# Side units ahead of the attention scores, eight gate units of layer 1 moved into retention and attention, and units in three passes

## The chip, the cores and the metric

One core of a Trainium2 chip runs the whole program. The metric is the device time of one execution in microseconds (us). The engines named here are PE (TensorE, the matrix multiplier), DVE (VectorE), ACT (ScalarE) and SP (SyncE, which only issues DMAs). Each engine works through its own queue strictly in order and waits on semaphores for the others. Matmul results go to eight PSUM banks.

## The reference, cut to what matters

Two networks follow each other. The first has two mixer layers with four branches each; in layer 0 the 256 tokens and the 256 context tokens are both needed (512 columns), in layer 1 mostly the 256 tokens (256 columns). The second network has an RG-LRU block, a gated FFN, a gated linear attention block and another FFN.

```python
for l in range(DEPTH):                       # DEPTH = 2
    px = split_proj(hx @ w_in[l])            # ret_*, sc_*, cf_*, att_*, merge_gates
    ret_x = retention_bidir(ret_q, ret_k * k_scale, ret_v, ...)
    att_x = windowed_gqa(rope(att_q), rope(att_k), att_v, ...)   # softmax(scores) @ v
    r = head_group_norm(ret_x) * silu(ret_z)
    s = short_conv(sc_b, sc_c, sc_x) * silu(sc_z)
    f = conformer_conv(cf_glu) * silu(cf_z)
    a = att_x * silu(att_z)
    merged = sum(sigmoid(g) * (br @ w_branch[i])
                 for i, (g, br) in enumerate(zip(gates, (r, s, f, a))))
    x = x + gate_x * (merged @ w_out[l])
# second network
x = x + gt_m * rmsnorm(mixer(h)); x = x + gt_f * rmsnorm(conv_ffn(h))   # twice
```

The gate `sigmoid(g)` has 4 x 1024 columns, 1024 for each branch; they depend on nothing but the layer's normalized input `hx`, so they can be projected as early as that is there. All of it is float32.

## The kernel before

**Units.** Every large projection is cut into units of 128 output columns. The weights come in slabs of two units (`ring`, 3 slabs, one DMA by SP each, in the order of the list `stream`). A unit's weights are split into a rounded part and the rest: `w_hi` is a copy on ACT (L1115), `w_lo` is `slab - w_hi` on DVE (L1729), and there are four buffers of each (`PARTS`), so that the split of unit u waits until PE has used unit u-4. The input is split in the same way (`h_hi`, `h_lo`). PE then makes three products for each of 8 tiles k of the contraction: `w_hi·h_hi` (L537), `w_hi·h_lo` (L538), `w_lo·h_hi` (L539), 24 matmuls per unit, interleaved by k. `unit()` waits at the start for both `w_hi` and `w_lo` of the unit; `open_bank` waits until what was in that bank eight openings ago has been emptied; `project` (L547) is the two and the 24 matmuls. Some calls of `project` also pass `ready`, a wait before each k for an input that is only just being made. ACT and DVE split ahead of use: `split_until(name)` is three units past `name` (`AHEAD`), and is called at fixed places in their queues.

**Clock keepers.** `keep_clock(n)` (L506, matmul at L512) puts n dummy matmuls of ones, each counted twice in the profile, where PE would have nothing to do.

**Retention** (layer l, loops over 4 heads). PE: scores of head n (L716), a unit where `in_ret` names one (none in layer 1; `keep_clock(8)` at n = 1), then the output of head n-1 (L726, L732), which waits for the decayed scores that DVE makes (L2075).

**Attention.** Eight tiles of 128 queries and two heads in layer 1 (16 in layer 0). In step i of its loop PE does scores of tile i+1 (L757), the first side unit of the step, the output of tile i-2 (L780), further side units, `keep_clock(11)` in step 1 of layer 1, and the turning of tile i-1 (L768, eight transposes). ACT does the exponentials of tile i (L1368), which also empty its score banks; then for each side unit the split of a later unit (L1115) and the evacuation of this one (L1101); then the evacuation of the turned tile i-1 (L1101). DVE does the band and row maximum of tile i (L2095, L2100), the w_lo for the side units (L1729), the weights of tile i-1 (L2126), and the store of output i-3 (L2133). So PE turns tile i-1 when DVE has made its weights, for which ACT has to have made its exponentials.

**Side units** are units that nothing in the stage needs: `side_tiles` (L454) shares out sc_b, sc_z, ret_z and att_z. In layer 1 eight of them run before retention and eight inside attention, one in each of steps 1 to 8 and none in step 0. In layer 0 four are before or in retention and 12 in attention.

**Merge.** For each branch in `MERGE_ORDER` (sc, ret, att, cf) there are 4 pairs: two gate units, then two branch units (4 tiles of k). ACT takes the sigmoid of each gate from its bank, DVE multiplies it with the branch product and adds. DVE also works off "blocks" here (L1766, the adaptive scales and shifts of the second network, 128x1024 each), as `mod_plan` shares them out by pair: in layer 1 two in each of the pairs 1 to 12, and later in the steps of the first FFN's down projection. SP loads them two slabs after the weights of their pair (`due`, L1078).

## Time and profile before

| | us |
|---|---|
| median of 3 runs | 1893.91 (1892.77 to 1894.66) |
| the profiled execution's own time | 1894.95 |
| its span | 1893.1 |
| PE busy | 1812.9 (96%) |
| PE weight loads busy | 1597.7 (84%) |
| DVE busy | 1436.2 (76%) |
| ACT busy | 885.8 (47%) |
| largest groups: L537, L538, L539 on `h_hi`, `h_lo` | 885.6, 875.4, 874.6 (2800 each) |
| mean granted TensorE clock | 0.992 |
| one block on DVE (L1766), mean | 1.28 |
| DVE busy from 1505.0 to 1514.5 (end of the first FFN's down projection) | 0.76 of 9.50 |

"Busy" is the time in which at least one instruction of the engine runs; the ends of matmuls are modelled, so a busy PE can still be fed more slowly than it could be. A timeline row gives the start, the duration, the engine, the line and operation, output <- inputs, shapes, the number of instructions folded into the row and, in brackets, how long the engine stood idle before it and who ended that. Layer 1's retention runs from about 921 to 938 us, its attention to 999 us, its merge from 1028 to 1163 us.

### The profile page before, as it was taken

The page shows a single profiled execution, that of the slowest core. Times are in us where ns is not written, and L with a number is a line of the kernel's source. Part 1 is how long each engine was busy: PE and PEld are TensorE (multiplying, and loading weights), DVE is VectorE, ACT ScalarE, POOL GpSimd, SP SyncE. Part 2 cuts the span into 40 slices and gives each one's busy share as a digit, 9 for nine tenths or more (in the row PEclk, how much of TensorE's full clock was granted, in tenths as well). Part 3 has the DMA queues.
Part 4 walks back from the last instruction along what each step waited for, and adds up shares of the span by engine and source line. Part 5 has one row for each costly group of instructions (what it writes and reads, how often), then busy time and mean ns, then how long its engine had stood idle before and what let it go on. Part 6 is the DMA issues. An engine that isn't in the chain of part 4 may idle for free.

```text
span 1893.1 us, 30016 instructions
## 1 busy us (share of the span) xinstructions
PE 1812.9 (96%) x11532; PEld 1597.7 (84%) x11532; DVE 1436.2 (76%) x2531; ACT 885.8 (47%) x1528; POOL 0.2 (0%) x4
## 2 busy tenths in 40 slices
PE   4999999999999999999999999998998999999997
PEld 2788886777888887988878999887998979989997
DVE  5649985458899987797767897676988788769863
ACT  3322334446322333443457455574655356556552
POOL 0000000000000000000000000000000000000000
PEclk8999999999999999999999999999999999999999
DMA  9422311113577776343223986342656924235542
GB/s 343 132 89 91 105 51 67 45 56 122 201 266 252 246 247 234 125 150 119 76 79 100 321 299 204 114 159 96 201 184 251 322 81 143 90 99 194 197 163 84
DMA packets 242909, 302.78 MB, mean 160 GB/s; under 512 B 6080, under 2 KB 224448, under 8 KB 242256
## 3 DMA queue, kind: packets, MB, share of 16 engines
q1 hardware_dynamic: 242768, 300.87, 47.4%
q8 instruction: 93, 1.52, 0.3%
q14 instruction: 48, 0.39, 0.1%
HBM read 299.79 MB, written 1.05 MB: 159 GB/s over the span
## 4 chain that ended last, share of the span: by engine, by line
PE 77%; DVE 12%; ACT 6%; issue 3%; DMA 1%; SPq 0%; DVEq 0%; ACTq 0%
PE bank L537 23%; PE bank L539 23%; PE bank L538 23%; DVE w_lo L1729 3%; ACT w_hi L1115 1%; PE bank L780 1%; ACT work L1101 1%; DVE work L2183 1%; PE bank L768 1%; DVE work L2315 1%; DVE work L2321 1%; DVE stats L1663 1%; PE bank L584 1%; DMA arena<-in_w_mod 1%; PE bank L880 1%
## 5 line engine op out<-in xcount | busy, mean ns | idle before, releaser
L537 PE MATMUL bank<-h_hi,w_hi 128*128 128x256 f32 (+2 forms) x2800 | 885.6, 316 | 32.4 <-DVE h_lo L1682 9.1
L538 PE MATMUL bank<-h_lo,w_hi 128*128 128x256 f32 (+2 forms) x2800 | 875.4, 313 | 0.0
L539 PE MATMUL bank<-h_hi,w_lo 128*128 128x256 f32 (+2 forms) x2800 | 874.6, 312 | 0.0
L1729 DVE TENSOR_TENSOR w_lo<-ring,w_hi 128x1024 fp32r<-128x1024 f32 (+2 forms) x444 | 500.1, 1134 | 219.4 <-ACT w_hi L1115 218.6
L537 PEld LDWEIGHTS bank<-h_hi,w_hi 128*128 128x128 f32 x2800 | 530.0, 189 | 81.4 <-issue 21.3
L539 PEld LDWEIGHTS bank<-h_hi,w_lo 128*128 128x128 f32 x2800 | 530.6, 189 | 31.8
L538 PEld LDWEIGHTS bank<-h_lo,w_hi 128*128 128x128 f32 x2800 | 528.4, 189 | 31.7 <-issue 0.7
L1115 ACT ACTIVATE w_hi<-ring 128x1024 fp32r<-128x1024 f32 (+2 forms) x444 | 434.4, 985 | 174.2 <-PE bank L539 142.2
L1101 ACT ACTIVATE work<-bank 128x512 f32<-128x512 f32 (+1 forms) x142 | 69.4, 507 | 274.6 <-PE bank L539 225.7
L1101 ACT ACTIVATE arena<-bank 128x256 f32<-128x256 f32 (+4 forms) x121 | 55.2, 457 | 241.9 <-PE bank L539 174.5
L537 PE MATMUL bank<-arena_r,w_hi 128*128 128x256 f32 (+2 forms) x464 | 153.3, 330 | 3.2 <-issue 1.5
L539 PE MATMUL bank<-arena_r,w_lo 128*128 128x256 f32 (+2 forms) x464 | 150.5, 324 | 0.0
L538 PE MATMUL bank<-arena_r,w_hi 128*128 128x256 f32 (+2 forms) x464 | 150.2, 324 | 0.0
L2005 DVE SCALAR_TENSOR_TENSOR arena<-arena,params 128x512 f32<-128x512 f32 (+1 forms) x240 | 130.5, 613 | 0.0
L1766 DVE CUSTOM_DVE_ANT_0 arena<-arena,c_row,params 128x1024 f32<-128x1024 f32 x96 | 120.7, 1281 | 10.0 <-DMA arena<-in_ada_w_t 9.8
L537 PEld LDWEIGHTS bank<-arena_r,w_hi 128*128 128x128 f32 x464 | 87.6, 189 | 12.8 <-issue 3.1
L538 PEld LDWEIGHTS bank<-arena_r,w_hi 128*128 128x128 f32 x464 | 87.6, 189 | 8.5 <-issue 1.2
L539 PEld LDWEIGHTS bank<-arena_r,w_lo 128*128 128x128 f32 x464 | 87.6, 189 | 7.8
L1101 ACT ACTIVATE work<-bank,params 128x256 f32<-128x256 f32 x88 | 49.7, 564 | 93.1 <-DVE w_lo L1729 57.3
L1762 DVE CUSTOM_DVE_ANT_0 arena<-arena,tables,params 128x1024 f32<-128x1024 f32 x48 | 60.6, 1282 | 18.6 <-DMA arena<-in_w_mod_t 18.6
L2315 DVE SCALAR_TENSOR_TENSOR work<-bank,params,work 128x255 f32<-128x255 f32 x88 | 42.3, 481 | 36.7 <-ACT work L1101 36.5
L512 PE MATMUL bank<-tables 128*128 128x256 f32 x280 | 63.0, 379 | 0.0
(242 smaller groups left out, 1552.1 us busy)
## 6 DMA issues: line engine op xcount, KB each, us to landing
ring<-in_w_in SPq DMA_DIRECT2D x86, 1024.0 KB, 5.2
arena<-in_ada_w_t SPq DMA_DIRECT2D x96, 512.0 KB, 6.2
ring<-in_ffn_w_up SPq DMA_DIRECT2D x44, 1024.0 KB, 5.1
ring<-in_w_branch SPq DMA_DIRECT2D x32, 512.0 KB, 4.6
arena<-in_w_mod_t SPq DMA_DIRECT2D x32, 512.0 KB, 5.3
ring<-in_ffn_w_down SPq DMA_DIRECT2D x16, 1024.0 KB, 5.3
ring<-in_gla_w_in SPq DMA_DIRECT2D x12, 1024.0 KB, 5.3
ring<-in_w_out SPq DMA_DIRECT2D x8, 1024.0 KB, 5.3
```

Of the source, the lines that this page charges most:

```text
L512: pe.matmul(psum[b % BANKS][:, 0:S], ones, tables[:, 0:S], start=True, stop=True)
L537: pe.matmul(out, ws[0][:, k, :], hi, start=start, stop=False)
L538: pe.matmul(out, ws[0][:, k, :], lo, start=False, stop=False)
L539: return pe.matmul(out, ws[1][:, k, :], hi, start=False, stop=stop)
L584: m = pe.matmul(out[0:2, 0:256], csil[:, k, 0:2], w[:, k, :], start=k == 0, stop=k == KT - 1)
L1101: return nc.scalar.activation(dst, src, func, **kw)\
L1115: nc.scalar.activation(w_hi[u % PARTS][:, 0:src.shape[1], :], src, ACT.Copy)\
L1729: step(nc.vector.tensor_tensor(w_lo[u % PARTS][:, 0:nk, :], src, w_hi[u % PARTS][:, 0:nk, :].bitcast(F32), ALU.subtract), f"lo {u}", *(["u ...
L1762: step(nc.vector.tensor_tensor_reduce(w if v else scratch, w, c_rows[:, v, :], 1.0, param("b_mod", 2)[:, l, c:c + 1], ALU.mult, ALU.add, m ...
L1766: step(nc.vector.tensor_tensor_reduce(w, w, c2_row, 1.0, param("ada_b", 2)[:, l, c:c + 1], ALU.mult, ALU.add, mod2[l][:, c:c + 1]), name)
L2005: step(nc.vector.scalar_tensor_tensor(dst, src, cw[:, l, k, n:n + 1], dst, ALU.mult, ALU.add), name)
L2315: step(nc.vector.scalar_tensor_tensor(acc[:, 1:S], src[:, 0:S - 1], fw[:, l, 1, c:c + 1], acc[:, 1:S], ALU.mult, ALU.add), f"tap1 {name}")
```

## The change

Five edits.

1. `project` without `ready` waits for `w_hi` alone, opens its bank, runs the eight `w_hi·h_hi`, then the eight `w_hi·h_lo`, then waits for `w_lo`, then runs the eight `w_lo·h_hi`. 363 units go this way: 218 of 256 columns, 18 of 258 and 127 of 512, some with four tiles of k (counted in triples of matmuls: 1632, 144 and 904). Calls with `ready`, `project_group` and the FFN's down projection are as before (584 triples).
2. In attention, both layers, the first side unit of a step stands ahead of the scores.
3. The last two of the eight gate units of each branch in layer 1 become side units. Layer 1's retention now has `ret_z 1.0` at n = 1 in place of `keep_clock(8)`, attention has 15 side units (steps 0 to 8: 1, 2, 2, 1, 2, 2, 1, 2, 2), and `keep_clock(11)` is gone. ACT evacuates the eight raw gates into unused halves of two arrays and takes the sigmoid from there in the merge, whose last pair of each branch has branch units only. Their slabs stand after att_z's in the stream.
4. The blocks of layer 1's merge: two in each pair whose number is not 3 modulo 4 (22 in all; 24 before), so none with the pairs without gate units; the two left over go to the last step of the FFN's down projection.
5. SP's `due` leaves the four early gate slabs out.

```diff
@@ mod_plan
-            mod_plan[1, pair] = take_blocks(adas, 2 if pair < 13 else 0)
+            mod_plan[1, pair] = take_blocks(adas, 2 if pair % 4 < 3 else 0)
@@ stream
-            for a in ("ret_z", "att_z", "cf_z"):
+            for a in ("ret_z", "att_z"):
                 for i in range(2):
                     section(l, a, i, run)
+            for b in MERGE_ORDER if l else ():
+                gate_slab(b, 3)
+            for i in range(2):
+                section(l, "cf_z", i, run)
@@ side_tiles
+            if l:
+                names += [f"gate {l}.{b}.{n}" for b in MERGE_ORDER for n in (KT - 2, KT - 1)]
-            first, mid = (2, (1, 3)) if l == 0 else (2 * BT, ())
+            first, mid = (2, (1, 3)) if l == 0 else (2 * BT, (1,))
@@ project (PE)
-                w = unit(name)
-                out = open_bank(name)
-                for k in range(tiles):
-                    if ready:
+                if ready:
+                    w = unit(name)
+                    out = open_bank(name)
+                    for k in range(tiles):
                         ready(k)
-                    m = three_products(out[:, 0:n], w, k, hi(k, n), lo(k, n), k == 0, k == tiles - 1)
+                        m = three_products(out[:, 0:n], w, k, hi(k, n), lo(k, n), k == 0, k == tiles - 1)
+                else:
+                    u = unit_of[name]
+                    pe.wait_ge(*scalar.did(f"hi {u}"))
+                    w = w_hi[u % PARTS], w_lo[u % PARTS], f"used unit {u}"
+                    out = open_bank(name)
+                    for k in range(tiles):
+                        pe.matmul(out[:, 0:n], w[0][:, k, :], hi(k, n), start=k == 0, stop=False)
+                    for k in range(tiles):
+                        pe.matmul(out[:, 0:n], w[0][:, k, :], lo(k, n), start=False, stop=False)
+                    pe.wait_ge(*vector.did(f"lo {u}"))
+                    for k in range(tiles):
+                        m = pe.matmul(out[:, 0:n], w[1][:, k, :], hi(k, n), start=False, stop=k == tiles - 1)
@@ attention (PE)
-                    if i + 1 < len(att):
-                        att_scores(i + 1)
                     side = in_step[i] if i < len(in_step) else []
                     for name in side[:1]:
                         project(name, nx)
+                    if i + 1 < len(att):
+                        att_scores(i + 1)
                     if i >= 2:
                         att_out(i - 2)
                     for name in side[1:]:
                         project(name, nx)
-                    if l and i == 1:
-                        keep_clock(11)
@@ merge (PE)
-                        for j in range(2):
+                        for j in range(2 if l == 0 or i < 3 else 0):
                             project(f"gate {l}.{b}.{2 * i + j}", nx)
@@ side_out (ACT)
+                    if name.startswith("gate"):
+                        b, n = name.split(".")[1:]
+                        evacuate(name, early_gate(b, int(n)), also=[f"gate raw {l}.{b}.{n}"])
+                        return
@@ merge (ACT)
+                        if l and n >= KT - 2:
+                            act.wait_ge(*scalar.did(f"gate raw {l}.{b}.{n}"))
+                            nc.scalar.activation(act_t[m % 4][:, 0:nx], early_gate(b, n), ACT.Sigmoid)\
+                                .then_inc(*scalar.does(f"gate {l}.{m}"))
@@ SP
-                if name.startswith(("w gate", "w branch")):
+                if name.startswith(("w gate", "w branch")) and not (name.startswith("w gate 1") and name.endswith(".3")):
```

The three places in the order of the instructions on which the prediction leans. First, PE at the start of layer 1's attention, before. L757 are scores (two matmuls per tile), L537 to L539 a unit, L512 the clock keeper, L768 the turning of a tile:

```order
L757 MATMUL bank<-arena 128x512 x6
L537 MATMUL bank<-h_hi,w_hi 128x256
L538 MATMUL bank<-h_lo,w_hi 128x256
L539 MATMUL bank<-h_hi,w_lo 128x256
L537 MATMUL bank<-h_hi,w_hi 128x256
L538 MATMUL bank<-h_lo,w_hi 128x256
L539 MATMUL bank<-h_hi,w_lo 128x256
...
L539 MATMUL bank<-h_hi,w_lo 128x256
L512 MATMUL bank<-tables 128x256 x11
L768 MATMUL bank<-tables,work 128x128 x8
L757 MATMUL bank<-arena 128x512 x2
```

and the same place now (L785 are the scores, L577, L579, L582 the passes of a unit, L796 the turning):

```order
L785 MATMUL bank<-arena 128x512 x2
L577 MATMUL bank<-h_hi,w_hi 128x256 x8
L579 MATMUL bank<-h_lo,w_hi 128x256 x8
L582 MATMUL bank<-h_hi,w_lo 128x256 x8
L785 MATMUL bank<-arena 128x512 x2
L577 MATMUL bank<-h_hi,w_hi 128x256 x8
L579 MATMUL bank<-h_lo,w_hi 128x256 x8
L582 MATMUL bank<-h_hi,w_lo 128x256 x8
L796 MATMUL bank<-tables,work 128x128 x8
```

Before, three tiles' scores, one unit and eleven dummies stand ahead of the first turning; now three tiles' scores and three units, with one more unit and no dummy. The unit rows are now runs of eight by pass.

Second, DVE at the same place, before. L2095 and L2100 are the maximum of a tile, L1729 is a w_lo, L2126 the weights of the first tile, for which PE's first turning waits:

```order
L2095 TENSOR_TENSOR bank<-bank,tables 128x128 x2
L2100 TENSOR_REDUCE small<-bank 128x1 x2
L2105 SCALAR_TENSOR_TENSOR small<-small 128x2
L2108 TENSOR_TENSOR small<-small,params 128x2
L1729 TENSOR_TENSOR w_lo<-ring,w_hi 128x1024
L2116 TENSOR_TENSOR small<-small 128x2
L2121 RECIPROCAL small<-small 128x2
L2126 TENSOR_SCALAR work<-work,small 128x512 x2
```

and now (L1763 is the w_lo, L2160 the weights):

```order
L1763 TENSOR_TENSOR w_lo<-ring,w_hi 128x1024
L2129 TENSOR_TENSOR bank<-bank,tables 128x128 x2
L2134 TENSOR_REDUCE small<-bank 128x1 x2
L2139 SCALAR_TENSOR_TENSOR small<-small 128x2
L2142 TENSOR_TENSOR small<-small,params 128x2
L1763 TENSOR_TENSOR w_lo<-ring,w_hi 128x1024 x2
L2150 TENSOR_TENSOR small<-small 128x2
L2155 RECIPROCAL small<-small 128x2
L2160 TENSOR_SCALAR work<-work,small 128x512 x2
```

Three w_lo now stand between the first tile's maximum and its weights, where one stood.

Third, PE in layer 1's retention, before. L716 are the scores, L726 and L732 the output:

```order
L716 MATMUL bank<-arena 128x256 x4
L512 MATMUL bank<-tables 128x256 x8
L726 MATMUL bank<-work,arena 128x256 x2
L732 MATMUL bank<-work,arena 128x256 x2
L716 MATMUL bank<-arena 128x256 x2
```

and now:

```order
L744 MATMUL bank<-arena 128x256 x4
L577 MATMUL bank<-h_hi,w_hi 128x256 x8
L579 MATMUL bank<-h_lo,w_hi 128x256 x8
L582 MATMUL bank<-h_hi,w_lo 128x256 x8
L754 MATMUL bank<-work,arena 128x256 x2
L760 MATMUL bank<-work,arena 128x256 x2
```

A unit of work stands where the eight dummies stood.

## Rows read from the trace of the kernel before

**Rows 1.** The page's first part: busy us, share of the span, instructions:

```profile
PE 1812.9 (96%) x11532; PEld 1597.7 (84%) x11532; DVE 1436.2 (76%) x2531; ACT 885.8 (47%) x1528; POOL 0.2 (0%) x4
```

**Rows 2.** Windows: us, busy us of each engine, granted clock, DMA share, GB/s:

```profile
975.00:1000.00 25.00, 23.22 (x198) 20.45 (x198) 14.22 (x40) 13.88 (x30) 0.00 (x0) 1.00 0.21 65
1075.00:1100.00 25.00, 25.00 (x214) 25.00 (x213) 23.00 (x40) 12.49 (x23) 0.00 (x0) 1.00 0.85 292
```

**Rows 3.** Timeline of PE, layer 0's attention (two of eight such waits):

```profile
310.81 0.43 PE L780 MATMUL bank<-work,arena 128*64 128x128 f32 x2 [0.41 <-ACT stats L1368]
...
346.73 0.47 PE L537 MATMUL bank<-h_hi,w_hi 128*128 128x512 f32 x1 [0.71 <-ACT work L1368]
```

**Rows 4.** Timeline of PE, layer 1's retention at n = 1:

```profile
924.48 3.62 PE L512 MATMUL bank<-tables 128*128 128x256 f32 x16
...
928.78 1.13 PE L726 MATMUL bank<-work,arena 128*128 128x256 f32 x4 [0.69 <-DVE work L2075]
```

**Rows 5.** Timeline of PE, layer 1's attention: its start and one whole step:

```profile
944.13 4.91 PE L512 MATMUL bank<-tables 128*128 128x256 f32 x22
948.88 0.49 PE L768 MATMUL bank<-tables,work 128*128 128x128 f32 x3
...
962.65 1.09 PE L768 MATMUL bank<-tables,work 128*128 128x128 f32 x8
963.67 1.13 PE L757 MATMUL bank<-arena 64*128 64x512 f32 x4
965.30 0.36 PE L537 MATMUL bank<-h_hi,w_hi 128*128 128x256 f32 x1 [0.50 <-ACT work L1368]
...
968.26 1.58 PE L780 MATMUL bank<-work,arena 128*64 128x128 f32 x16
969.78 0.33 PE L768 MATMUL bank<-tables,work 128*128 128x128 f32 x1
```

**Rows 6.** Timeline of ACT in that step:

```profile
963.40 1.08 ACT L1101 ACTIVATE work<-bank 128x512 f32<-128x512 f32 x2 [1.77 <-PE bank L768]
964.37 0.69 ACT L1368 ACTIVATE work<-bank,small 128x512 f32<-128x512 f32 x1
...
965.79 1.07 ACT L1115 ACTIVATE w_hi<-ring 128x1024 fp32r<-128x1024 f32 x1
```

**Rows 7.** Timeline of DVE in that step:

```profile
966.90 1.23 DVE L1729 TENSOR_TENSOR w_lo<-ring,w_hi 128x1024 fp32r<-128x1024 f32 x1 [2.53 <-ACT w_hi L1115]
...
968.43 0.88 DVE L2126 TENSOR_SCALAR work<-stats,small 128x512 f32<-128x512 f32 x2
...
969.82 1.28 DVE L2100 TENSOR_REDUCE small<-bank 128x1 f32<-128x512 f32 x2
```

**Rows 8.** Windows around a stall of PE in the first FFN's down projection:

```profile
1458.50:1461.50 3.00, 0.48 (x5) 0.31 (x4) 2.96 (x6) 0.78 (x3) 0.00 (x0) 1.00 1.07 384
1461.50:1465.00 3.50, 3.50 (x18) 3.50 (x18) 2.80 (x4) 2.00 (x2) 0.00 (x0) 0.51 1.07 375
```

**Rows 9.** Timeline, PE and DVE where stages start:

```profile
461.84 0.47 PE L537 MATMUL bank<-h_hi,w_hi 128*128 128x512 f32 x1 [0.64 <-ACT w_hi L1115]
...
1031.68 2.39 DVE L1729 TENSOR_TENSOR w_lo<-ring,w_hi 128x1024 fp32r<-128x1024 f32 x2 [0.66 <-DVE arena L2153]
...
1033.01 0.36 PE L537 MATMUL bank<-h_hi,w_hi 128*128 128x256 f32 x1 [1.57 <-ACT w_hi L1115]
...
1280.83 0.36 PE L537 MATMUL bank<-h_hi,w_hi 128*128 128x256 f32 x1 [1.89 <-issue]
```

**Rows 10.** Timeline of PE: two matmuls 756 apart in layer 1's merge:

```profile
1060.00 0.28 PE L537 MATMUL bank<-h_hi,w_hi 128*128 128x256 f32 x1
...
1149.42 0.28 PE L537 MATMUL bank<-arena_r,w_hi 128*128 128x256 f32 x1
```

**Rows 11.** Timeline of PE, a unit's first matmuls after a wait:

```profile
958.17 0.36 PE L537 MATMUL bank<-h_hi,w_hi 128*128 128x256 f32 x1 [0.61 <-ACT stats L1368]
958.37 0.28 PE L538 MATMUL bank<-h_lo,w_hi 128*128 128x256 f32 x1
```

More of the change, by code:

```diff
@@ L244, in program, with early_gate @@
         branch_lo = dict(ret=parts_of(6384), sc=parts_of(2288), cf=parts_of(4336), att=parts_of(0))
+        def early_gate(b, n):
+            i = 2 * MERGE_ORDER.index(b) + n % 2
+            return (att_o if i < BT else s_br)[:, i % BT, S:2 * S]
         x1_hi, x1_lo = (arena_r[:, c:c + KT * LATE_N].rearrange("p (t s) -> p t s", t=KT)
@@ L2213, in _ @@
                             low_parts(b)
-                        if n % 2 == 0:
+                        with_gates = n % 2 == 0 and not (l and n >= KT - 2)
+                        if with_gates:
                             split_for(f"gate {l}.{b}.{n}")
```

18 lines of the change are left out of this document (11 added, 7 removed).

## The prediction

> **What bounds the kernel now.** The first part of the page says PE: 96% busy [rows 1]. Next I asked in two windows whether busy is full: in layer 1's merge 25 us hold 214 matmuls of 256 columns, in layer 1's attention 198 [rows 2]. Two starts 756 matmuls apart lie 89.42 us apart, 0.1183 us each [rows 10]; that is the price of a matmul, and a full unit of 24 costs 2.84. Work moved from one saturated stage to another is worth nothing. A gain must come from time in which PE is not saturated: waits, dummies, stage starts. The reader should see in the timeline rows where these stand in brackets. In the merge DVE is busy 23.00 of 25 us [rows 2], so it is the engine behind PE there.
>
> Layer 1's attention is not bounded by PE. One step is 969.78 - 962.65 = 7.13 us [rows 5]. The ring: PE turns (0.97), ACT evacuates the two halves (963.40 to 964.37), does the exponentials (the unit's bank is freed only by them, hence 0.50 idle), then PE runs the unit (2.96) and the output (1.52), and turns again [rows 5, 6]. PE's own work in it is turn 1.02, scores 0.95, unit 2.9, output 1.52, together 6.4. The remaining 0.7 is slack that more or reordered PE work can use.
>
> **The change part by part.** The sum is made on the profiled execution (1894.95; span 1893.1), which lies 1.04 above the median; I put the change on the median.
>
> *Side unit ahead of the scores, layer 0.* Eight waits of PE there are for a bank that the exponentials free, four of 0.41 ahead of an output and four ahead of a unit (two of 0.50, two of 0.71), 4.06 in all [rows 3]. With the unit first, the scores (about 1 us) and the unit change places, and each bank is asked for that much later relative to the exponentials that free it; the next late thing would be DVE's weights, which have no wait of PE there now. **-4.0**; bounds 0 (all come back) and -4.06.
>
> *Retention, layer 1.* The eight dummies (3.62) and the wait behind them (0.69 for DVE's scores) [rows 4] become a unit of 2.84. PE alone would win 1.5. But DVE now has a w_lo (1.23) [rows 7] and ACT a w_hi (1.07) and an evacuation (under the 0.54 of each 512-wide one) [rows 6] in the chain of decay and scores that the next outputs wait for. I take **+1.5** for the end of retention; bounds -1.4 and +2.7.
>
> *Attention, layer 1, start.* From retention's end (939.9 by the line above) PE has three scores (0.95 each) and three units (2.9): ready for the first turning at 951.4. The chain is longer. DVE's maximum of tile 0 ends 942.9 (1.28 for two, and small steps of 0.7 before and behind it [rows 7]), then exponentials to 944.5, w_hi to 945.5, w_lo to 946.7, maximum of tile 1 to 948.7, exponentials and two w_hi with evacuations to 952.4, w_lo to 953.7, weights (0.88 and two small steps) to 954.9. So PE turns at 955.0 and idles **3.6 us** in one piece, where dummies of 4.91 kept it occupied [rows 5] (the turning was at 948.88). In the trace a stall like this is followed by the lower level: 0.48 busy in 3 us, then 0.51 granted for the next 3.5 us [rows 8], which is 1.2 GHz instead of 2.4. Half of 3.5 us is lost: **+1.75** (bounds 0, if the level stays, and 3.5).
>
> By the Trainium skill ("TensorE: Matmul & The Clock Gate", on the clock gate) an idle PE loses its clock and dense work is what keeps it, which is a rule against taking both keepers away. The row above agrees in direction. Without the drop the sum would be 1.75 lower.
>
> *Attention, the rest.* A step with one unit is now PE's own 6.4 (the bank wait is gone), one with two units 6.4 + 2.9 = 9.3. Steps 2 to 6 have 2, 1, 2, 2, 1 units: 9.3 + 6.4 + 9.3 + 9.3 + 6.4 = 40.7. One more wait: in step 5 the second unit's bank is that of an output which DVE stores only after the next weights, 1.7. Steps 7 and 8 have two units and no scores, 8.35 each; the last output 1.5 with a wait of 0.4. From 956.0 (end of the first turning): + 42.4 + 16.7 + 1.9 = 1017.0, against 998.7 before: **+18.4**, of which seven further units are 20.4. Unsure by 3 up (DVE and ACT have two splits in many steps) and 2 down.
>
> *Merge, layer 1.* 192 matmuls go: 192 x 0.1172 = **-22.5**. The gates' splits go too, and DVE's multiplication is no worse off. At the end I add 1.4: the last pair of gates with blocks is now pair 14, so DVE (23.00 of 25 [rows 2]) comes later to the low parts of `merged`, for which the output projection waits. Bounds 0 and 3. Four parts of layer 1 so far: +18.4 (with retention's 1.5 inside, as it starts from 939.9) + 1.75 - 22.5 + 1.4 = **-1.0**. The moved blocks cost 2 x 1.28 on DVE in the last down step; DVE is busy 0.76 us in the 9.5 behind it, so I take 0.
>
> *Three passes, starts.* Where a stage starts, the first unit waits for w_lo; with the new order it starts on w_hi, one w_lo (about 1.2) earlier, and the w_lo has 16 matmuls (1.9 us) to arrive. Layer 0's merge: the wait is 0.64 and all of it goes, -0.6. Layer 1's: 1.57 at 1033.01; w_lo's pair begins 1031.68, so the first unit can begin about 1.4 sooner, -1.4. The stage behind the RG block: the wait is 1.89 at 1280.83, of which the first w_lo (1.2) goes, and a wait of the same kind 6 us earlier gives the rest; -2.05 together [rows 9]. Sum **-4.05**; bounds -4.6 and 0. At layer 1's start, where ACT and DVE feed units more slowly than PE takes them, the gain is absorbed: 0. Elsewhere the trace shows no wait at a unit's start, and a wait that is long fulfilled is priced next.
>
> *Three passes, spacing.* Between 1060 and 1149 the step L537 to L538, which keeps the same weights, is 0.1171, the two others 0.1186 and 0.1192 (252 each, first and last in [rows 10]). In passes every matmul changes its weights: 3 x (0.1189 - 0.1183) = 1.8 ns a triple, x 1776 triples of 256 and 258 columns = **+3.1**. The 512-column matmuls show no such difference. The bounds: 0, and +3.3; or, if passes of one form run at the shortest step, 1776 x 3.6 ns = -6.
>
> By the same page's section on back-to-back matmuls a weight load is pulled ahead under the running matmul, so that the order would be free. Then the sum would be 3.1 lower.
>
> Sum: -4.0 - 1.0 - 4.05 + 3.1 = **-6.0**, 1893.9 - 6.0 = **1887.9**.
>
> **The rivals.**
> *A, cleaner.* No drop of the clock, spacing unchanged, DVE in time at the merge's end: 1887.9 - 1.75 - 3.1 - 1.4 = 1881.6. For it: the merge is saturated and the 512-column rows show no weight effect. Against it: the stall is longer than that of [rows 8].
> *B, absorbed.* Attention's chain on ACT and DVE is longer than my hand count (two splits, two evacuations and an exponential in one step), or layer 0's waits come back as waits for DVE's weights. 2 of the 4 us return there, and 3 in layer 1: 1893. For it: 2.53 us is all DVE's slack ahead of its w_lo in a step of one unit [rows 7], and a second costs 1.23.
> *C, slower.* The wait in the middle of each unit stops PE from fetching the next weights, though it is long fulfilled. After a real wait the step from the first matmul to the second is 0.20 (958.17 to 958.37) against 0.117 [rows 11]: +0.08 x 363 units = +29, 1917. It decides from 6.0 / 363 = 0.017 us per unit. Against it: between two units there are waits of the same kind now, long fulfilled, and the 89.42 us of [rows 10] hold no gap at them.
> *D, the change doesn't do what it says:* the early gates' raw values leave ACT late, so that the merge's last pairs wait. ACT is busy 12.49 of 25 us there [rows 2] and the gates are done 20 us earlier; hardly possible, and counted in B.
>
> **How the numbers follow.** Forecast as worked out, 1887.9: 0.50 (with its bounds 1884 to 1892). A: 0.22. B: 0.20. C: 0.05; others, 0.03. The range of 8 in 10 reaches from below A's half, 1880.5, to just above B, 1893.5. About 0.2% (3.8 us) can be told from no change, so faster begins below 1890.1: all of A, four fifths of the forecast's chance and little of B: 0.67. Same, to 1897.7: 0.25. Slower: 0.08.
>
> **What would show it.** Right: no bank wait of PE in layer 0's attention; PE's turn of tile 0 in layer 1 about 955, after an idle of 3 to 4 us, and a window at 0.50 clock behind it; attention's end near 1017 and the merge's work 192 matmuls shorter; layer 1's merge starting on ACT's w_hi; a mean step of 0.1189 in the merge. Wrong: waits of 0.5 or more inside two-unit steps (B), a gap of 0.05 or more between pass two and three of each unit (C), or a clock that never falls (A). If layer 0's attention and the stage starts keep their waits, the whole -8 fails and the kernel is no faster.

## The result: 10 us faster

The changed kernel takes 1883.66 us (median of 4 runs, 1883.57 to 1884.62), the kernel before 1893.85 beside it (one run more than in the table of before): ratio 0.9948, 95% interval 0.993 to 0.9965. That is 10.2 us faster. The forecast was 1887.9, so the direction and the range held, and the size was about 4 us short. The profiled execution took 1883.57, its span is 1881.8 (1893.1 before).

The page's first part for the changed kernel, as [rows 1] for before:

```profile
PE 1804.0 (96%) x11494; PEld 1592.6 (85%) x11494; DVE 1436.6 (76%) x2531; ACT 887.0 (47%) x1536; POOL 0.2 (0%) x4
```

PE is busy 8.9 us less, at practically the same number of matmuls (38 fewer: the 19 dummies, each counted twice). DVE does the same work, ACT eight instructions more (the sigmoids of the moved gates). Busy shares say little more; what tells is where the same instruction stands in both traces. The table follows PE's work that both kernels share: the difference (after minus before) that each stretch added, beside the forecast.

| stretch, by the time in the trace of before | forecast | measured |
|---|---|---|
| start to 49 us | 0 | -1.74 |
| 49 to 438: layer 0 up to and with attention | -4.0 | -5.89 |
| 438 to 739: layer 0's merge and output | -0.6 | -1.33 |
| 739 to 916: layer 1's input projections | 0 | +1.29 |
| 916 to 1024: its retention and attention | +20.15 | +19.97 |
| 1024 to 1177: its merge and output | -22.5 | -21.58 |
| 1177 to 1295: RG block | -2.05 | -3.10 |
| 1295 to 1479: first FFN | 0 | -1.67 |
| 1479 to the end | 0 | +2.75 |
| spacing of matmuls, over all | +3.1 | in the rows above |
| sum | -5.9 | -11.3 |

The trace beats the sum by 5.4 us. Of that 3.1 are the spacing term, which did not come, 1.9 layer 0's attention, 1.0 the RG block, 0.7 layer 0's merge and 0.2 layer 1's attention; layer 1's merge gives 0.9 back. The four rows with a forecast of 0 (-1.74, +1.29, -1.67, +2.75) come to +0.6 together. That they nearly cancel is luck, as the next sections show.

Layer 1's attention, the part with the longest working, came out almost to the number, though its parts did not. The timeline of PE in the changed kernel, to be read against [rows 5]: start, duration, line, operation, and in brackets the idle time before it. L785 are scores, L796 a turning, L577 a unit's first pass, L808 an output:

```profile
931.98 0.70 PE L785 MATMUL bank<-arena 64*128 64x512 f32 x2
...
946.52 1.97 PE L796 MATMUL bank<-tables,work 128*128 128x128 f32 x8 [2.22 <-DVE work L2160]
...
957.33 0.27 PE L796 MATMUL bank<-tables,work 128*128 128x128 f32 x1
...
964.27 0.30 PE L796 MATMUL bank<-tables,work 128*128 128x128 f32 x1 [0.51 <-DVE arena L2167]
...
973.59 0.27 PE L796 MATMUL bank<-tables,work 128*128 128x128 f32 x1
...
981.76 0.36 PE L577 MATMUL bank<-h_hi,w_hi 128*128 128x256 f32 x1 [1.73 <-DVE arena L2167]
...
984.67 0.28 PE L796 MATMUL bank<-tables,work 128*128 128x128 f32 x1
...
1009.58 0.29 PE L808 MATMUL bank<-work,arena 128*64 128x128 f32 x1 [0.40 <-ACT work L1126]
```

The first turning waits 14.5 us behind the first scores (forecast 15.1) and idles 2.22. The three scores and three units ahead of that turning took 12.3 us (931.98 to 944.30), where the hand count had 11.5. The step from 964.27 to 973.59 has two units and takes 9.3, as forecast; the one from 973.59 to 984.67 has the wait for the stored output, 1.73 where the forecast had 1.7. What the hand count did not have are 0.51 and 0.52 in two one-unit steps (before the turnings at 964.27 and 991.62), again for something that DVE stores late (L2167).

### The profile page after: what moved, and what is told of

Same layout as the page of the kernel before. It is cut to its first block, busy times and chain, and to the rows that moved or that the text cites. A ratio compares the mean times of both kernels' runs of the same rounds, so it can differ in the third digit from the quotient of the medians.

```text
span 1881.8 us, 29899 instructions
## 1 busy us (share of the span) xinstructions
PE 1804.0 (96%) x11494; PEld 1592.6 (85%) x11494; DVE 1436.6 (76%) x2531; ACT 887.0 (47%) x1536; POOL 0.2 (0%) x4
## 4 chain that ended last, share of the span: by engine, by line
PE 41%; DVE 10%; ACT 5%; issue 2%; DMA 1%; DVEq 0%; ACTq 0%
PE bank L577 9%; PE bank L582 9%; PE bank L579 9%; DVE w_lo L1763 3%; PE bank L553 3%; PE bank L555 3%; PE bank L554 3%; ACT w_hi L1140 2%; PE bank L992 1%; ACT work L1126 1%; PE bank L905 1%; DVE work L2350 1%; DVE stats L1697 1%; DVE work L2356 1%; DVE arena L2318 1%
## 5 line engine op out<-in xcount | busy, mean ns | idle before, releaser
L1763 DVE TENSOR_TENSOR w_lo<-ring,w_hi 128x1024 fp32r<-128x1024 f32 (+2 forms) x444 | 499.4, 1133 | 208.4 <-ACT w_hi L1140 205.2
L577 PE MATMUL bank<-h_hi,w_hi 128*128 128x256 f32 (+2 forms) x2374 | 424.1, 321 | 3.8 <-DVE arena L2167 1.7
L582 PE MATMUL bank<-h_hi,w_lo 128*128 128x256 f32 (+2 forms) x2374 | 411.8, 315 | 1.2 <-DVE w_lo L1763 1.2
L579 PE MATMUL bank<-h_lo,w_hi 128*128 128x256 f32 (+2 forms) x2374 | 412.4, 316 | 0.0
L577 PEld LDWEIGHTS bank<-h_hi,w_hi 128*128 128x128 f32 x2374 | 348.5, 189 | 40.9 <-issue 4.9
L582 PEld LDWEIGHTS bank<-h_hi,w_lo 128*128 128x128 f32 x2374 | 347.5, 189 | 31.1 <-DVE w_lo L1763 1.4
L579 PEld LDWEIGHTS bank<-h_lo,w_hi 128*128 128x128 f32 x2374 | 348.1, 189 | 29.9
L1126 ACT ACTIVATE arena<-bank 128x256 f32<-128x256 f32 (+3 forms) x129 | 58.3, 453 | 245.1 <-PE bank L582 171.9
L553 PE MATMUL bank<-h_hi,w_hi 128*128 128x256 f32 (+2 forms) x426 | 128.7, 302 | 23.6 <-DVE h_lo L1716 9.1
L1800 DVE CUSTOM_DVE_ANT_0 arena<-arena,c_row,params 128x1024 f32<-128x1024 f32 x96 | 120.6, 1280 | 11.7 <-DMA arena<-in_ada_w_t 11.3
L554 PE MATMUL bank<-h_lo,w_hi 128*128 128x256 f32 (+2 forms) x426 | 125.4, 294 | 0.0
L555 PE MATMUL bank<-h_hi,w_lo 128*128 128x256 f32 (+2 forms) x426 | 125.3, 294 | 0.0
L553 PEld LDWEIGHTS bank<-h_hi,w_hi 128*128 128x128 f32 x426 | 81.9, 192 | 29.6 <-issue 13.1
L555 PEld LDWEIGHTS bank<-h_hi,w_lo 128*128 128x128 f32 x426 | 82.0, 192 | 1.8
L554 PEld LDWEIGHTS bank<-h_lo,w_hi 128*128 128x128 f32 x426 | 81.7, 192 | 1.6
L577 PE MATMUL bank<-arena_r,w_hi 128*128 128x512 f32 (+2 forms) x306 | 65.9, 341 | 0.4 <-ACT w_hi L1140 0.4
```

Of the source, the lines that this page charges most:

```text
L553: pe.matmul(out, ws[0][:, k, :], hi, start=start, stop=False)
L554: pe.matmul(out, ws[0][:, k, :], lo, start=False, stop=False)
L555: return pe.matmul(out, ws[1][:, k, :], hi, start=False, stop=stop)
L577: pe.matmul(out[:, 0:n], w[0][:, k, :], hi(k, n), start=k == 0, stop=False)
L579: pe.matmul(out[:, 0:n], w[0][:, k, :], lo(k, n), start=False, stop=False)
L582: m = pe.matmul(out[:, 0:n], w[1][:, k, :], hi(k, n), start=False, stop=k == tiles - 1)
```

## The granted clock does a part of it, and by chance

I looked next for the stretches at the lower level. Windows of the changed kernel (us, busy of each engine, granted clock, DMA share, GB/s), to be read with [rows 8]:

```profile
816.00:820.00 4.00, 4.00 (x12) 3.15 (x11) 4.00 (x9) 0.00 (x0) 0.00 (x0) 0.57 0.10 17
946.50:949.50 3.00, 2.98 (x14) 2.98 (x15) 2.28 (x7) 1.57 (x3) 0.00 (x0) 0.50 0.89 309
1448.80:1452.00 3.20, 3.20 (x27) 3.20 (x28) 2.50 (x4) 2.01 (x2) 0.00 (x0) 1.00 1.07 372
1526.50:1529.50 3.00, 3.00 (x16) 3.00 (x16) 0.47 (x2) 2.97 (x6) 0.00 (x0) 0.50 0.03 5
1577.50:1581.00 3.50, 3.50 (x18) 3.50 (x19) 3.47 (x5) 0.85 (x1) 0.00 (x0) 0.53 0.08 22
1676.00:1680.50 4.50, 4.50 (x27) 4.50 (x27) 3.88 (x10) 2.10 (x5) 0.00 (x0) 0.62 0.17 53
```

Apart from the kernel's very start and end, these are five stretches at 1.2 GHz; by the rows of traces with and without one, each is worth 1.4 to 1.6 us. The trace of before has two, at 1461 [rows 8] and at 1540. The third window is the place of [rows 8]: the same stall, now 1.91 instead of 2.52 (the one ahead of it 1.90 instead of 1.48), and no drop. Most of the first FFN's -1.67 is that drop. The windows at 1577 and 1676 are the two halves of the +2.75 behind 1479. The one at 816 is the +1.29 of layer 1's start (in the traces of five and six below, which have none there, that row is -0.3). In the second network the diff changes nothing but the passes and two blocks, and at the start of the kernel nothing at all. Yet the start gives -1.74, and between -0.5 and -1.5 in the traces of the other kernels below. It is the clock too: the level is at 1.2 GHz from 34.7 to 48.4 us in the trace of before and from 34.9 to 45.1 in that of the changed kernel. In the same 2.8 us the first starts 8 matmuls and the second 14:

```profile
45.50:48.30 2.80, 2.80 (x8) 2.15 (x7) 2.80 (x6) 0.00 (x0) 0.00 (x0) 0.50 1.10 348
```

```profile
45.50:48.30 2.80, 2.80 (x14) 1.76 (x13) 2.80 (x7) 0.00 (x0) 0.00 (x0) 1.00 1.10 348
```

Half of the 3.3 us between the two ends is the 1.7 of this row; in the trace of the passes alone (experiment three) the level rises at 47.5, and the row is -0.47. So a large part of the table's right column might be luck, and the experiments had to separate that from the edits.

## Experiments: the three edits apart

**One: the passes undone.** `project` as before, the rest as changed.

```diff
-                if ready:
...
+                w = unit(name)
+                out = open_bank(name)
+                for k in range(tiles):
+                    if ready:
+                        ready(k)
+                    m = three_products(out[:, 0:n], w, k, hi(k, n), lo(k, n), k == 0, k == tiles - 1)
```

> The changed kernel with the three passes undone (24 matmuls interleaved by k again, both parts of the weights awaited at the start); order and gates as changed. Theory: passes are worth the shorter waits where stages start (0.64 at layer 0's merge, 1.4 at layer 1's, 1 to 2 behind the RG block) and some tenths of a nanosecond per matmul, less the clock that the trace of after shows at half level from 816 to 820 us, where PE idles 1.96 us in one piece (0.69 before). So this kernel takes 1886 to 1888 us, shows no half level at 816, and layer 1's merge starts with a wait of 1.5. Rival: passes cost as much at every matmul as I put in the forecast (+3.1), so that taking them away changes nothing: 1883 to 1885.

Measured: 1887.38 (1884.05 to 1890.11), ratio 0.996 (0.9948 to 0.9973); all ratios are to the kernel before, timed beside the run. No half level stands at 816, and layer 1's merge starts with a wait of 1.59:

```profile
1045.81 0.36 PE L553 MATMUL bank<-h_hi,w_hi 128*128 128x256 f32 x1 [1.59 <-ACT w_hi L1128]
```

against this in the changed kernel:

```profile
1043.98 0.39 PE L577 MATMUL bank<-h_hi,w_hi 128*128 128x256 f32 x1 [0.97 <-ACT w_hi L1140]
```

As the theory said; the passes are worth having. By the medians it is 3.7 us, but the ratio's interval overlaps that of the changed kernel (0.993 to 0.9965), so the weight rests on these rows.

**Two: the order in attention alone,** on the kernel before.

```diff
-                    if i + 1 < len(att):
-                        att_scores(i + 1)
                     side = in_step[i] if i < len(in_step) else []
                     for name in side[:1]:
                         project(name, nx)
+                    if i + 1 < len(att):
+                        att_scores(i + 1)
```

> The kernel before with the first side unit ahead of the scores in both layers' attention, nothing else. Theory: layer 0 gains 5.3, more than the 4.06 of the idle in brackets, since each wait also lengthens the matmul behind it (0.07 for 128 columns, 0.25 for 512); layer 1 gains 0.6 in each of about five steps, since PE's own work of a step is 6.4 against the ring's 7.13. Time 1885 to 1887. Rival: layer 1's steps are a ring of ACT and DVE that the order does not shorten: 1888 to 1889, step still 7.1 us.

Measured: 1887.35 (1886.41 to 1890.97), ratio 0.9967 (0.9957 to 0.9978). Layer 0 up to the end of attention gains 5.91 in this trace, the same as in the changed kernel (5.89): the whole of that row is the order. Layer 1 gains 0.32 only. Two turnings in a row there:

```profile
961.84 0.33 PE L768 MATMUL bank<-tables,work 128*128 128x128 f32 x1 [0.23 <-DVE work L2125]
...
968.79 0.33 PE L768 MATMUL bank<-tables,work 128*128 128x128 f32 x1 [0.23 <-DVE work L2125]
```

The step is 6.95 (7.13 before), and the wait is now for DVE's weights, not for a bank. With one unit per step layer 1's attention is a ring through ACT and DVE. The rival was right for layer 1, the theory for layer 0, which gave even more than its 5.3.

**Three: the passes alone,** on the kernel before.

```diff
+                    for k in range(tiles):
+                        pe.matmul(out[:, 0:n], w[0][:, k, :], hi(k, n), start=k == 0, stop=False)
+                    for k in range(tiles):
+                        pe.matmul(out[:, 0:n], w[0][:, k, :], lo(k, n), start=False, stop=False)
+                    pe.wait_ge(*vector.did(f"lo {u}"))
...
```

> The kernel before with the three passes alone. Theory: the stage starts give 3 to 4, the start of layer 1 gives its gain back and adds a clock drop of 1.75: 1890 to 1892. Rival: if passes cost 1.8 ns per triple as forecast, the merge of 256 columns shows steps of 0.1189 and the time is 1893 to 1895.

Measured: 1888.16 (1885.28 to 1891.38), ratio 0.9969 (0.9959 to 0.9978): faster than expected. Its trace gives -1.25 for layer 0's merge, -2.0 for layer 1's, -1.50 at the start of the RG block's output, and +1.27 for layer 1's start, where it has the half level, too.

**Four: no gate moved,** order and passes on the kernel before, dummies and blocks as they were (experiments two and three together).

> The kernel before with the order in attention and the three passes, but no gate moved, the dummies and the blocks as before. Theory: moving the gates exchanges 22.5 us of saturated merge for 20 us of attention and loses 2.9 at the end of the merge (PE waits 0.94 and 1.67 for the parts of merged) and 1.75 to a clock drop behind the first turning; so without it the kernel is as fast or faster than the changed one: 1881 to 1884. Rival: the gates carry the gain, since they fill the ring's slack in layer 1's attention: 1887 or more.

Measured: 1881.74 (1881.25 to 1883.01), ratio 0.9937 (0.9922 to 0.9952). As the theory said, the kernel without the moved gates is no slower than the changed one. Its median is 1.9 lower, but the ratios overlap, and against run twelve below (0.9935) there is no difference. From 916 to 1177 its trace gains 2.47, the changed kernel's 1.61. Moving 22.7 us of units (8 of 2.84) from the merge cost 20.4 in retention and attention, so 2.3 of slack was recovered there in spite of a half level of 1.5; then the merge gave 19.5 back, not 22.7, for it now has the tail that experiment five looks at.

**Ten (of the later runs): the passes with both waits in front.** It separates the order of the matmuls from the earlier start.

```diff
                     pe.wait_ge(*scalar.did(f"hi {u}"))
+                    pe.wait_ge(*vector.did(f"lo {u}"))
...
-                    pe.wait_ge(*vector.did(f"lo {u}"))
                     for k in range(tiles):
                         m = pe.matmul(out[:, 0:n], w[1][:, k, :], hi(k, n), start=False, stop=k == tiles - 1)
```

> The changed kernel with its three passes in order, but with both parts of the weights awaited at the start of the unit. Theory: the passes have two effects, the earlier start and a slightly shorter step in stages with large matmuls; only the first goes here: layer 0's merge stage gains 0.6 to 0.7 over the kernel before instead of 1.3, layer 1's merge start 0.6 instead of 2, the time is 1885 to 1886. Rival: the wait in the middle of the unit costs something by itself, so that without it the dense stretches are faster and the total is the same or below 1883.7.

Measured: 1884.54 (1884.18 to 1885.95). Layer 0's merge gains 0.33 where the changed kernel gains 1.33: the earlier start is 1.0 of it (a wait of 0.66 and its restart), the order 0.3. The start of the RG block's output gains 0.21 against 1.49. On the spacing, windows of 50 us inside layer 1's merge, of before, of this kernel, and of the changed kernel; the number behind PE's busy time counts its matmuls:

```profile
1060.00:1110.00 50.00, 50.00 (x425) 50.00 (x424) 45.74 (x78) 24.90 (x42) 0.00 (x0) 1.00 0.88 304
```

```profile
1060.00:1110.00 50.00, 50.00 (x428) 50.00 (x427) 44.79 (x77) 27.77 (x49) 0.00 (x0) 1.00 0.87 297
```

```profile
1060.00:1110.00 50.00, 50.00 (x427) 50.00 (x427) 45.89 (x80) 27.81 (x48) 0.00 (x0) 1.00 0.90 303
```

425, 428 and 427: passes are a little denser, not less dense. One matmul more or less is the edge of a window (the kernel of experiment one, interleaved, shows 426); over 70 us of starts (1060 to 1130) the mean step is 0.1183 in the three interleaved kernels (before, one and two) and 0.1176 or 0.1177 in all eleven with passes. In the first FFN (1320 to 1420) it is 0.1183 in all of them. Between this kernel and the changed one lies only the wait in the middle of a unit, and the step does not show it, so rival C (a wait in mid-unit that costs even when long fulfilled) is out.

## Experiments: the end of the merge, and the clock

**Five: the two blocks of pair 14 to the down projection's third and fourth steps.**

```diff
-            mod_plan[1, pair] = take_blocks(adas, 2 if pair % 4 < 3 else 0)
+            mod_plan[1, pair] = take_blocks(adas, 2 if pair % 4 < 3 and pair < 14 else 0)
-            mod_plan[2, i] = take_blocks(adas, 3 if i < 2 else 2)
+            mod_plan[2, i] = take_blocks(adas, 3 if i < 4 else 2)
```

> The changed kernel with the two blocks of layer 1's pair 14 moved to the first FFN's down projection. Theory: the waits of PE for the parts of merged at the end of layer 1's merge (0.94 and 1.67, with their restarts 2.9 us over the kernel before) come from DVE being behind by these blocks, 1.28 each; without them 2 to 3 us go: the end of the output projection is 2 to 3 earlier relative to its start, total 1881 to 1882 if no other clock drop appears (each of those is 1.75 and moves the total by itself). Rival: the waits come from the gates taken from the side arrays or from ACT, so nothing changes: waits 0.9 and 1.7 stay.

The end of the merge in the changed kernel, PE's two waits in the output projection and DVE before them (L1800 is a block, L2270 the last additions to `merged`):

```profile
1153.21 0.35 PE L553 MATMUL bank<-h_hi,w_hi 128*128 128x256 f32 x1 [0.94 <-ACT h_hi L1455]
...
1155.48 0.36 PE L553 MATMUL bank<-h_hi,w_hi 128*128 128x256 f32 x1 [1.67 <-ACT h_hi L1455]
```

```profile
1146.07 1.28 DVE L1800 CUSTOM_DVE_ANT_0 arena<-arena,c_row,params 128x1024 f32<-128x1024 f32 x1
...
1150.72 1.22 DVE L1763 TENSOR_TENSOR w_lo<-ring,w_hi 128x1024 fp32r<-128x1024 f32 x1 [1.09 <-ACT w_hi L1140]
...
1152.31 0.43 DVE L2270 TENSOR_TENSOR arena<-arena,work 128x256 f32<-128x256 f32 x1
...
1152.99 1.22 DVE L1763 TENSOR_TENSOR w_lo<-ring,w_hi 128x1024 fp32r<-128x1024 f32 x1
...
1154.57 0.42 DVE L2270 TENSOR_TENSOR arena<-arena,work 128x256 f32<-128x256 f32 x1
```

Measured: 1882.57 (1881.16 to 1883.79). The first wait is gone, the second stays at 1.64; the merge is 1.1 shorter (22.70 against 21.58), not 2 to 3. So the blocks are one cause of the tail. What else lies on the way is in the rows: DVE waits 1.09 for ACT's w_hi ahead of the last but one addition, and makes a whole w_lo of 1.22 between the last two. No run separates these. And DVE's debt came back later. The stall in the down projection, in this kernel:

```profile
1447.72 0.55 PE L553 MATMUL bank<-h_hi,w_hi 128*128 128x256 f32 x1 [3.55 <-DVE w_lo L1763]
```

3.55 where the changed kernel had 1.91 (2.47 in its second trace, run twelve), with a long half level around it; in seven, which has the same blocks there, it is 3.70. Moving a block to a place where DVE is the bound only moves the wait.

The same trace holds the most telling pair for the clock. Its windows behind layer 1's ret_k and behind the first turning:

```profile
816.20:820.20 4.00, 4.00 (x18) 3.26 (x19) 4.00 (x9) 0.11 (x1) 0.00 (x0) 1.00 0.18 58
946.00:950.00 4.00, 4.00 (x34) 3.87 (x36) 2.17 (x7) 3.01 (x8) 0.00 (x0) 1.00 0.64 222
```

and the idle time in front of each, in the same kernel:

```profile
816.14 0.47 PE L553 MATMUL bank<-h_hi,w_hi 128*128 128x512 f32 x1 [1.96 <-ACT arena L1126]
...
945.91 0.33 PE L796 MATMUL bank<-tables,work 128*128 128x128 f32 x1 [2.22 <-DVE work L2160]
```

1.96 and 2.22, exactly as in the changed kernel, and full clock behind both. The same idle piece drops the clock in one execution and not in another.

**Six: eight dummies ahead of the first turning.**

```diff
+                    if l and i == 1:
+                        keep_clock(8)
                     if 1 <= i <= len(att):
                         att_turn(i - 1)
```

> The changed kernel with eight dummies (1.9 us) in front of layer 1's first turning, inside the 2.22 us that PE stood idle there. Theory: the half level from 946 to 950 does not appear, the turning starts at the same time or within 0.2, and the end of attention is 1.5 to 1.9 earlier. Rival: the level falls anyway, because what went before was too thin, or the dummies push the turning: end of attention unchanged or later.

```profile
943.78 3.61 PE L528 MATMUL bank<-tables 128*128 128x256 f32 x16
947.23 0.49 PE L796 MATMUL bank<-tables,work 128*128 128x128 f32 x3
```

Measured: 1883.47 (1882.11 to 1885.57). No half level there, but the dummies last 3.45 and not 1.9, and push the turning by about 1.1. I had counted the rows of a dummy as dummies; [rows 4] has the right price, 3.62 for eight. The stretch is 1.0 longer than without dummies and without a drop (19.53 against 18.51), and 0.4 shorter than with the drop (19.97).

**Seven and eight: dummies in four more places, with and without the moved gates** (7 ahead of layer 1's ret_k, 19 for 11 in both FFNs, 20 for 12 ahead of gla z, 4 in the first level products; seven has the edits of five and six too).

> Both edits above together, and dummies in four more idle stretches of PE: ahead of ret_k in layer 1 (7, idle 1.96), in both FFNs ahead of the up projection (19 where 11 stood, idle 2.14), ahead of the gla z projection (20 where 12 stood, idle 2.10) and inside the first level products (4, idle 1.36). Theory: half levels at 816, 946, 1526, 1577 and 1676 us (1.5 to 1.75 each) go, with the blocks' 2 to 3: 1873 to 1877. Rival: half levels only move to other places, since they come with other idle pieces as well: 1879 to 1883.

> The kernel without moved gates (order and passes alone) with the same dummies in the same four stretches. Theory: with the clock kept in both, moving the gates is worth what the fill recovered (22.7 us of work in place of 18.6), so this kernel is 2 to 4 slower than the one before it in this list: 1877 to 1879. Rival: the gates bring nothing even then, the two are within 1 us.

Measured: 1884.02 (1883.2 to 1885.94) and 1883.74 (1881.9 to 1885.76), both well above what was expected. The half levels in the guarded places are gone, but each guard is 0.8 to 1.2 too long, as in six. With this overhead they can't tell the gates' worth.

**Nine and eleven: the dummies fitted, with and without the moved gates;** nine has the two blocks in the very last step of the down projection.

```diff
-            mod_plan[2, i] = take_blocks(adas, 3 if i < 2 else 2)
+            mod_plan[2, i] = take_blocks(adas, 3 if i < 2 else 2 if i < 4 * DOWN - 1 else 4)
+                if l:
+                    keep_clock(4)
+                    if l and i == 1:
+                        keep_clock(4)
-                keep_clock(11)
+                keep_clock(15)
-            keep_clock(12)
+            keep_clock(16)
+                    if n == 0 and half:
+                        keep_clock(2)
```

> The changed kernel with the two blocks of pair 14 in the very last step of the FFN's down projection (four there), and dummies sized by what eight of them took before the first turning (3.45 us, 0.43 each): 4 before the first turning, 4 ahead of ret_k in layer 1, 15 where 11 stood in the FFNs, 16 where 12 stood ahead of gla z, 2 in the first level products. Theory: none of these pushes the work behind it (within 0.1 us), no half level stands behind the five places, and the two blocks cost nothing in the last step: 1878 to 1880.5. Rival: the half level moves to the stalls of the down projection and the RG block as often as before: 1881 to 1884.

> The kernel without moved gates (order and passes alone) with the same fitted dummies at the four places it shares with the kernel above. Theory: with the clock held in both, the moved gates are worth their recovered slack, 1.5 to 3 us from retention to the output projection: 1880.5 to 1882. Rival: no difference between the two within 0.5 us, the gates bring nothing.

Measured, both as their theories said: nine 1878.64 (1875.83 to 1879.33), ratio 0.9919 (0.9906 to 0.9931); eleven 1881.29 (1880.95 to 1883.04), ratio 0.9938 (0.9926 to 0.995). In nine the turning comes after 0.49 of idle at 945.45, the stall of the down projection is back to 1.63, and the windows behind the guarded places are at full clock:

```profile
945.45 0.33 PE L798 MATMUL bank<-tables,work 128*128 128x128 f32 x1 [0.49 <-DVE work L2166]
...
1445.59 0.36 PE L553 MATMUL bank<-h_hi,w_hi 128*128 128x256 f32 x1 [1.63 <-DVE w_lo L1769]
```

```profile
816.00:820.00 4.00, 4.00 (x19) 3.24 (x18) 4.00 (x9) 0.00 (x0) 0.00 (x0) 1.00 0.05 16
945.00:949.00 4.00, 3.55 (x31) 3.55 (x32) 2.70 (x8) 2.48 (x7) 0.00 (x0) 1.00 0.70 239
1214.00:1216.50 2.50, 2.50 (x7) 2.01 (x6) 0.00 (x0) 2.49 (x6) 0.00 (x0) 0.50 0.00 0
```

One is left in the RG block at 1214. Eleven does worse on this count: its trace has half levels at 1217 and 1449, where nothing guards, and one at 1527, behind the 16 dummies ahead of gla z. From 916 to 1177 nine gains 4.27 and eleven 2.51, so with the clock held and the tail shortened the moved gates are worth about 1.8, of which 1.1 is the shortened tail (five). As the change made them they bring 0.6 where the level holds (18.5 - 21.6 = -3.1 against -2.5) and cost 0.9 where it falls, so nearly all of the gain is the order and the passes. The medians stand 2.7 apart, but the intervals of the ratios overlap a little. Nine is the fastest kernel of the study.

**Twelve: the changed kernel again.**

> The changed kernel itself once more, beside the three above on the same chip. If the half levels fall by chance from run to run, its trace shows them at other places than 816, 946, 1526, 1577 and 1676 us, while every stage without one takes the same time within 0.1 us; if they belong to the kernel, they are at the same places. Time 1882 to 1885 in either case.

Measured: 1883.12 as the median of six, but from 1877.81 to 1885.2. The two runs below 1880 had a mean granted clock of 0.994, the one at 1885.2 had 0.990. In the profiled one the idle pieces are the old ones, and the half levels partly at other places:

```profile
1155.00:1161.00 6.00, 5.17 (x24) 5.20 (x25) 4.44 (x14) 4.81 (x8) 0.00 (x0) 0.50 0.27 96
1452.00:1455.00 3.00, 3.00 (x14) 3.00 (x15) 2.28 (x4) 2.00 (x2) 0.00 (x0) 0.50 1.07 372
...
1577.50:1587.00 9.50, 7.89 (x67) 7.49 (x66) 7.72 (x9) 5.37 (x8) 0.00 (x0) 1.00 0.54 170
1678.00:1684.00 6.00, 5.51 (x47) 5.54 (x48) 5.09 (x13) 3.04 (x7) 0.00 (x0) 1.00 0.33 104
```

1155 and 1452 are new, those at 1577 and 1676 are gone, those at 816, 946 and 1530 recur. Stages without one agree within 0.1 us between the two traces of the same kernel. The start is 0.35 apart, since the clock rose at 45.6 here and at 45.1 there. The row of the first FFN, -1.67 in the table, is -0.07 here: the stall of the down projection is 2.47, and the level fell behind it.

Over all traces: behind the idle piece of 1.96 at layer 1's ret_k the level fell in 4 of 6, behind the 0.7 of the kernels without the earlier start in 0 of 4, with dummies in 0 of 4. Behind the 2.2 to 2.3 at the first turning it fell in 4 of 5, with dummies in 0 of 9. Behind the 2.14 ahead of the second FFN in 2 of 10, with more dummies in 0 of 4. Behind the longest stall of the down projection (1.6 to 3.7) in 8 of 14. One place is different: after the 2.10 ahead of gla z the level fell in 10 of 10, though up to 10 us behind the piece's end, with work of PE in between; with more dummies it fell in 1 of 4 (eleven). There only the place is a matter of chance.

## Why the prediction was right in range and short in size

- *Layer 0's attention: right mechanism, term too small.* Forecast -4.0, measured -5.9, the order alone; all eight bank waits are gone. I summed the idle in brackets. A wait costs more than its bracket. In the trace of before, two neighbouring outputs, and the same two in the changed kernel:

```profile
329.88 0.32 PE L780 MATMUL bank<-work,arena 128*64 128x128 f32 x1
...
333.95 1.58 PE L780 MATMUL bank<-work,arena 128*64 128x128 f32 x16 [0.41 <-ACT work L1368]
```

```profile
326.54 0.32 PE L808 MATMUL bank<-work,arena 128*64 128x128 f32 x1
...
330.13 0.32 PE L808 MATMUL bank<-work,arena 128*64 128x128 f32 x1
```

  4.07 became 3.59: 0.48 for a bracket of 0.41. Ahead of a unit of 512 columns a bracket of 0.50 was worth 0.74 (320.06 to 329.88 became 317.46 to 326.54). The eight waits give 5.3 in this way, 0.2 more are a shorter wait ahead of the first turning (1.24 became 1.03), and 0.4 lie in stretches without a bracket and are not explained.
- *Retention: right.* +1.5 forecast; its end moved from 7.67 to 6.43 earlier, +1.24.
- *Attention in layer 1: right mechanism, +20.15 against +19.97, so close by luck.* The idle at the first turning was 2.22 instead of 3.6 and the half level cost 1.46 (19.97 against 18.51 in five) instead of 1.75; against that the work ahead of the turning took 0.8 longer, and two waits of 0.5 were not counted. The sum put the half level as certain; it is a matter of chance, 4 times in 5.
- *Merge in layer 1: right within 1.* The removed work is there (the forecast took 0.1172 for a matmul, its own price of 0.1183 makes it 22.7), and so is the start's gain (waits of 1.12 and 1.57 became 0.38 and 0.97). The tail was put at 1.4 and was 2.6 of idle, 2.9 with restarts; denser passes paid something under 1.
- *Stage starts: right mechanism.* Layer 0's merge 1.3 against 0.6, by the same restart cost and the density. The RG block's output 1.5 against 2.05: 1.21 of the wait moved into the middle of the unit, since w_lo was more than 16 matmuls late. The RG block's row has 1.6 more in its first part. 0.6 of it is again such a start (a wait of 0.45 ahead of a unit at 1242.72, gone with the passes). The other 1.2 is this wait for DVE in the trace of before, which the changed kernel does not have:

```profile
1223.03 0.48 PE L914 MATMUL bank<-arena,ring 128*128 128x256 f32 x1 [1.27 <-DVE arena L2362]
```

- *Spacing: wrong, the step that failed.* +3.1 was derived from the three steps of a triple (0.1171, 0.1186, 0.1192) on the reading that a change of weights lengthens the step. In passes all matmuls change weights, and the mean step became 0.1176 in the merge where it was 0.1183, and stayed 0.1183 in the FFN. So the term was nothing, or a gain of about 1. The rows of before already spoke against the reading: among the 512-column matmuls (500 to 690 us) the step that keeps its weights is the longest, 0.2293 against 0.2284 and 0.2282. The Trainium skill ("TensorE: Matmul & The Clock Gate", "Back-to-back issue gap") says that the loads of weights and the matmuls are pipelined with each other; the prediction's inference from it, that the order would be free, is nearer to what was measured.
- *The clock at large: not in the forecast.* Half levels in places I never looked at moved the profiled execution by -1.74 (start), -1.67 and +2.75, and layer 1's start by +1.6. The last is an effect of the passes by way of chance: PE gets ahead by the early start, so it waits 1.96 in one piece instead of 0.69 and small ones.
- *The rivals.* A (1881.6, no drop) is what executions with few drops show and better (1877.8); B did not happen as a whole, though its mechanism bounds layer 1 at one unit per step; C is out.

At equal mean clock the two kernels compare like this. At 0.994 nine executions of the kernel before took 1891.2 to 1893.6, two of the changed kernel 1877.8 and 1878.1; at 0.993 twelve took 1892.6 to 1895.7 and one 1882.7; at 0.991 six took 1894.5 to 1896.2 and four 1883.5 to 1883.7. The edits are thus worth 11 to 14 us (a step of 0.001 in the mean clock is itself about 1.9 us, 0.001 of the span). The rows without half levels say the same: -5.9 - 1.3 - 0.3 + 18.5 - 21.6 - 3.1 = -13.7. The medians stand 10.2 apart, so 1 to 4 are given back through more frequent half levels.

What stays open: what decides whether one and the same idle piece drops the clock; and the wait for DVE in the RG block's first part: it is 1.33 in eight, 1.02 in eleven, 0.94 in two, about 0.25 in one and ten, and under 0.2 in the others, and no run isolates what sets it. With it set aside, the edits are worth 1.2 less.

## What to carry to other kernels

Read where the same instruction stands in both traces, stretch by stretch; edits that act in separate stages then add up to a tenth of a microsecond, while totals scatter by several. Price a wait of TensorE at its bracket plus the restart of the matmul behind it (0.07 for 128 columns and 0.25 for 512 here). Before making a stage start earlier or taking out filler work, ask into how long a single idle piece the remaining wait will gather, and size fillers by their measured duration, since a filler that is too long gives most of what it saves away again (1.0 of 1.5 in experiment six).

## What the runs showed of the hardware

- The granted clock fell to 1.2 GHz behind idle pieces of 1.9 to 2.3 us in some traces and not in others, for the same piece at the same place (1.96: 4 of 6; 2.14: 2 of 10); behind pieces of at most 0.7 us at layer 1's ret_k it never fell (0 of 4). It can also fall where no single piece is long: in eleven at 1527, with none over 0.5 in the 7 us ahead. Each fall costs 1.4 to 1.6 us, and the changed kernel's times spread over 7.4 us (1877.81 to 1885.2), the fast ones at a mean clock of 0.994, the slowest at 0.990.
- The stretch at 1.2 GHz near the kernel's start ended between 45.1 and 48.4 us in the fourteen traces, though nothing there was changed; it moved what follows by half the difference (-1.74 at 45.1, -0.47 at 47.5).
- A semaphore wait in the middle of 24 matmuls that is long fulfilled costs nothing that dense work would show (a mean step of 0.1176 us with it and 0.1177 without).
- In layer 1's merge, eight matmuls in a row on the same kind of operand run slightly denser than the interleaved triple (0.1176 against 0.1183 us), in the FFN equally dense (0.1183).
